# Input projection of a hybrid decoder layer: the left 240 token columns of each slot in two matmuls per K tile instead of three, with a VectorE add

## The chip, the cores and the metric

The kernel runs on one core of one Trainium2 chip, as one launch. The metric is the device time of a launch in microseconds (us). Before the change, three runs took 860.97, 862.88 and 862.4 us, a median of 862.4 us.

## The reference, cut to what matters

One decoder layer over 512 prompt tokens and 8 decode tokens, width 1024. The change touches only the first product, the input projection, whose columns feed an attention branch (q, k, v) and an RWKV branch:

```python
def token_mixer(x, x_prev_row, k_cache, v_cache, wkv0, w_in, ...):
    x_ext = jnp.concatenate([x_prev_row[:, None, :], x], axis=1)
    proj = x_ext @ w_in
    cur = proj[:, 1:]
    q = cur[..., :ATT_WIDTH]...; k = ...; v = ...
    rw_cur = cur[..., 3 * ATT_WIDTH:]
    rw_prev = proj[:, :-1, 3 * ATT_WIDTH:]
    rw = rw_cur + (rw_prev - rw_cur) * mu_shift
```

All tensors are fp32. Everything behind it (attention, the RWKV scan, output projection, layer norms, the convolutional FFN) is left alone.

## The kernel before

Activations lie channel-major: 128 channels on the partitions, tokens along the free dimension. The input projection works on `XC` = 528 token columns (512 prompt, 8 decode and their 8 previous rows) and `KT` = 8 K tiles. It goes through `N_IN` = 27 **slots**; a slot is one tile of 128 output channels. `SLOTS` sets the order: "a" slots give an attention tile, written to `att`; "r" slots give an RWKV tile, written to `pre` and then mixed with its neighbour column by `shift` into `rw`.

fp32 accuracy is had from the fast type fp32r by splitting both operands: `w_hi` is the weight rounded to fp32r by ScalarE, `w_lo` the rest, made by VectorE (`w_low`); `x_hi` and `x_lo` are the same for the activations. Each product is the sum of three: w_hi x_hi + w_hi x_lo + w_lo x_hi. A slot's 528 columns are two halves of 264; a half takes 8 K tiles of 3 matmuls of 264 columns, all accumulated in one PSUM bank (`banks[:, g % 3]`, g = 2 * slot + half). So the projection is 27 x 2 x 8 x 3 = 1296 matmuls.

What sets the order: every engine runs its own list, written by hand as loops over the slot number s, and the lists meet at semaphores.

- TensorE: `in_product(s)` runs the left half, then the right half. Between K tiles, `beside(half, i)` slips in small work of other stages: `scores`, `probs_t`, `values` (attention), `v_tokens` (slots 10, 12, 16, 20: transposes of the v tile), `low_rank`, `key_sums`, `key_spread`. A half waits until the bank that it takes over has been copied out (`in_copied`), and a slot for `w_lo` (`w_lo_ready`).
- ScalarE: in iteration s it copies out the right half of slot s-1 (`evac(s - 1, 1)`), makes `w_hi` of slot s+1, does the attention's copies, copies out the left half of slot s (`evac(s, 0)`), and then the exponentials (`att_exp`).
- VectorE: in iteration s it runs `shift(s - 1)` if that slot is an "r" slot, `w_low(s + 1)`, `mix_lo` every fourth slot, and then what belongs to the slot: `decay_sums`, `key_norm`, and from slot 10 on `soft` (score scaling and maxima) and `scale` (softmax division), with `transform` in slots 10, 14, 18 and 22. An iteration starts when the one before has ended: the engine is in order.

The SyncE list streams weights; it is not near the limit here. The small matmuls in `beside` use plain fp32; only the split products use fp32r.

Of the kernel before, what the change touches and what calls it, by code (L numbers as in the profile page):

```python
# [27 lines left out]
CC = AW // P  # L28
XC = T + 2 * B
XH = XC // 2  # L30
TC = T + B
TH = TC // 2
ALPHA = 2.0 ** 0.25
# [122 lines left out]
def layer(nc, a):  # L156
# [59 lines left out]
    onemka = sb(mixer, "onemka", [P, CC])  # L216

    pa = ExitStack()
    x_hi = sb(pa, "x_hi", [P, KT, XC], F32R)
    x_lo = sb(pa, "x_lo", [P, KT, XC], F32R)  # L220
    ksq = sb(pa, "ksq", [P, 2, XC])
    edec = ksq[:, :, 0:NCH * (CH + 1)].rearrange("p i (n t) -> p i n t", n=NCH)
    kbig = sb(pa, "kbig", [P, XC])
# [103 lines left out]
    w_hi_ready = sem("w_hi_ready")  # L327
    w_lo_ready = sem("w_lo_ready")
    w_late_ready = sem("w_late_ready")
    slot_used = sem("slot_used")  # L330
    sel_landed = sem("sel_landed")
    half_used = sem("half_used")
    const_landed = sem("const_landed")
# [3 lines left out]
    x_hi_ready = sem("x_hi_ready")  # L337
    x_lo_ready = sem("x_lo_ready")
    in_copied = sem("in_copied")
    rw_ready = sem("rw_ready")  # L340
    pre_zero = sem("pre_zero")
    v_tok_ps = sem("v_tok_ps")
# [181 lines left out]
    def _(sp):  # L524
# [72 lines left out]
        for s in range(2, N_IN):  # L597
            if s in (16, 20, 24):
                bias(s // 2 - 6)
                bias(s // 2 - 5)  # L600
            weights(s)
            if s == 6:
                sp.wait_ge(lora_ps, CC)
                sp.dma_start(low_up[:], a["bsel"]).then_inc(bsel_landed, 16)
            if s == 25:
                sp.wait_ge(in_copied, 2 * v_slots[-1] + 2)
                sp.dma_start(a["att_out"], att[:, CC:3 * CC, :]).then_inc(att_left, 16)

        sp.wait_ge(n_spread, CC)
# [2 lines left out]
        sp.wait_ge(w_lo_ready, N_IN)  # L612
        for v in range(2):
            sp.dma_start(swk[64 * v:64 * v + 64], a["swkv"][:, 32 * v:32 * v + 32, :]).then_inc(wkv_landed, 16)
        sp.wait_ge(slot_used, N_IN)
        sp.wait_ge(rw_ready, N_RW)
        sp.wait_ge(qb_done, 4 * CC)
        sp.wait_ge(a_mix_hi, CC)
# [72 lines left out]
    @block.gpsimd  # L691
    def _(pool):
        own = settled(pool)
        def w_low(l):
            n, s = k_tiles(l), N_IN + l
            hi, lo = w_at(l)
            pool.wait_ge(w_hi_ready, s + 1)
            pool.tensor_tensor(lo[:, 0:n * P], w_raw[:, s % 2, 0:n * P], hi[:, 0:n * P].bitcast(F32), ALU.subtract)\  # L698
                .then_inc(w_late_ready, 1)
            own(w_late_ready)  # L700

        pool.memset(pre[:, :, 0:1], 0.0).then_inc(pre_zero, 1)
        own(pre_zero)

        pool.wait_ge(slot_used, N_IN)
        for r in range(NKV):
            pool.memset(kv[96:P, r * NSB * AW:(r + 1) * NSB * AW], 0.0).then_inc(kv_zero, 1)  # L707
            own(kv_zero)

        def products(b):  # L710

            r = b % NKV
            pool.wait_ge(kv_landed[r], 64 * (b // NKV + 1))
            pool.wait_ge(q_landed[b % 2], 16 * (b // 2 + 1))
            rows = kv[:, r * NSB * AW:(r + 1) * NSB * AW].rearrange("p (t n) -> p t n", t=NSB)
            pool.tensor_tensor(rows, rows, qs[:, b % 2, :].unsqueeze(1).broadcast_to([P, NSB, AW]), ALU.mult)\
                .then_inc(q_used, 1)
            own(q_used)
            x = kv[:, r * NSB * AW:(r + 1) * NSB * AW].rearrange("p (g d) -> p g d", d=HD)
            pool.tensor_tensor(x[:, :, 0:HD // 2], x[:, :, 0:HD // 2], x[:, :, HD // 2:HD], ALU.add).then_inc(s_prod, 1)  # L720
            own(s_prod)

        def keys(q):
            return svec[:, q, :].unsqueeze(1).broadcast_to([P, 32, HD])

        def vals(x):
            return x.unsqueeze(2).broadcast_to([P, 32, HD])

        def step(out, a0, a1, op):
            pool.tensor_tensor(out, a0, a1, op).then_inc(sw_a, 1)  # L730
            own(sw_a)

        for b in range(NKV):
            products(b)
        pool.wait_ge(wkv_landed, 32)
        pool.wait_ge(sv_landed, 12 * 16)
        step(swt[:, :, :], swk, keys(4), ALU.mult)
        step(swk, swk, keys(1), ALU.mult)
        for b in range(NKV, B):
            products(b)  # L740
        pool.wait_ge(sw_sa, 1)
        step(swt[:, :, :], vals(ssa[:, 0, :]), keys(5), ALU.mult)
        step(swk, swk, swt[:, :, :], ALU.subtract)
        step(swt[:, :, :], vals(sval[:, :]), keys(2), ALU.mult)
        step(swk, swk, swt[:, :, :], ALU.add)
        step(swt[:, :, :], swk, keys(0), ALU.mult)

        def gate_parts(u):

            pool.wait_ge(gn_gs, u + 1)  # L750
            if u >= 2:
                pool.wait_ge(gn_o, u - 1)
            if u == 1:
                pool.wait_ge(s_sum, 1)
            w = P if u < TB else B
            pool.tensor_tensor(unit(gw_gate[:, u % 2, 0, :], u), unit(gsb, u),
                               par[:, C_GW:C_GW + CC].unsqueeze(2).broadcast_to([P, CC, w]), ALU.mult).then_inc(gn_g, 1)
            own(gn_g)
            pool.tensor_tensor(unit(gw_gate[:, u % 2, 1, :], u), unit(gsb, u), unit_of(rw[:, J_V:J_V + CC, :], u), ALU.mult)\
                .then_inc(gn_g, 1)  # L760
            own(gn_g)

        def odd_low(half, i):

            pool.wait_ge(ln_hi, KT * half + 2 * i + 2)
            pool.wait_ge(ln_zv, 2 * half + i // 2 + 1)
            x = slice(2 * i, 2 * i + 2)
            pool.tensor_tensor(x1_lo[:, x, span(half)], z[:, x, span(half)], x1_hi[:, x, span(half)].bitcast(F32),
                               ALU.subtract).then_inc(ln_lo_odd, 1)
            own(ln_lo_odd)  # L770

        pool.wait_ge(y_landed, 32)
        w_low(0)
        w_low(1)
        pool.wait_ge(vb_done, CC)
        gate_parts(0)
        gate_parts(1)
        w_low(2)
        gate_parts(2)
        w_low(3)  # L780
        w_low(4)
        gate_parts(3)
        w_low(5)
        w_low(6)
        gate_parts(4)
        for l in range(7, L_FF + 2):
            w_low(l)
        odd_low(0, 1)
        odd_low(0, 3)
        w_low(10)  # L790
        w_low(11)
        odd_low(1, 1)
        odd_low(1, 3)
        for l in range(L_FF + RING, N_LATE):
            w_low(l)
# [3 lines left out]
    def _(ac):  # L799
        own = settled(ac)  # L800
        def w_high(s):
            ac.wait_ge(w_landed[s % 2], 16 * (s // 2 + 1))
            if s >= 2:
                ac.wait_ge(slot_used, s - 1)
            ac.activation(w_hi[:, s % 2, :], w_raw[:, s % 2, :], ACT.Copy).then_inc(w_hi_ready, 1)
            own(w_hi_ready)

# [32 lines left out]

        def evac(s, half):
            kind, i = SLOTS[s]
            if half == 0:
                ac.wait_ge(half_used, s + 1)
            else:
                ac.wait_ge(slot_used, s + 1)
            lo = half * XH
            if kind == "a":
                if half == 0:
                    ac.wait_ge(x_lo_ready, KT)  # L850
                out = att[:, i, lo:lo + XH]
            else:
                r = RW_SEQ.index(i)
                if r >= 2:
                    ac.wait_ge(rw_ready, r - 1)
                if r == 0:
                    ac.wait_ge(pre_zero, 1)
                out = pre[:, r % 2, 1 + lo:1 + lo + XH]
            ac.activation(out, banks[:, (2 * s + half) % 3, 0:XH], ACT.Copy).then_inc(in_copied, 1)
            own(in_copied)  # L860

        def v_tok_copy(c):
# [143 lines left out]
        ac.wait_ge(ends_in, 2 * CC)  # L1006
        ac.activation(dec[:, :, :], dec[:, :, :], ACT.Exp, scale=DEC).then_inc(ends_done, 1)
        own(ends_done)
        ac.wait_ge(slot_used, N_IN)
        ac.wait_ge(a_mix_lo, CC)  # L1010
        rows_copy(0)
        x0_copy(0, 0)
# [222 lines left out]
    def _(ve):  # L1235
# [28 lines left out]
        link(ve.memset(kbig[:, 0:NCH * (CH + 1):CH + 1], 0.0))  # L1264
        link(ve.memset(cum[:, :, :, 0:1], 0.0))

        def shift(s):

            j = SLOTS[s][1]
# [73 lines left out]
        for s in range(N_IN + 1):  # L1343
            if s == 1:
                ve.wait_ge(const_landed, 16 * N_CONST)
                link(ve.tensor_scalar(onemka[:, :], par[:, C_KA:C_KA + CC], -1.0, 1.0, ALU.mult, ALU.add))
            if 1 <= s < N_IN and SLOTS[s - 1][0] == "r":
                shift(s - 1)
            if s + 1 < N_IN:
# [160 lines left out]
            ve.tensor_reduce(ssa[:, i, :], swt[:, :, :], AX, ALU.add).then_inc(sw_y if i else sw_sa, 1)  # L1510
            own(sw_y if i else sw_sa)

        ve.wait_ge(slot_used, N_IN)
        mix_lo(CC - 1)
        ve.wait_ge(ends_done, 1)
        inverse_start(0, 0)
# [362 lines left out]
    def _(pe):  # L1879
# [3 lines left out]
        def in_product(s, beside):  # L1883

            pe.wait_ge(w_lo_ready, s + 1)
            for half in range(2):
                g = 2 * s + half
                if g >= 3:
                    pe.wait_ge(in_copied, g - 2)
                out, cols = banks[:, g % 3, 0:XH], slice(half * XH, (half + 1) * XH)  # L1890
                for i in range(KT):
                    wh, wl = (w[:, s % 2, i * P:(i + 1) * P] for w in (w_hi, w_lo))
                    if g < 2 and i % 2 == 0:
                        pe.wait_ge(x_lo_ready, 4 * g + i // 2 + 1)
                    mm(out, wh, x_hi[:, i, cols], i == 0, False)
                    mm(out, wh, x_lo[:, i, cols], False, False)
                    ins = mm(out, wl, x_hi[:, i, cols], False, i == KT - 1)
                    if i < KT - 1:
                        beside(half, i)
                ins.then_inc(slot_used if half else half_used, 1)  # L1900

        def v_tokens(c):

            pe.wait_ge(in_copied, 2 * v_slots[c] + 2)
            if c == 0:
                pe.wait_ge(kk_ap, CC)
            else:
# [377 lines left out]
            ins.then_inc(bt_ps, 1)  # L2285

        pe.wait_ge(in_copied, 2 * N_IN)
        pe.wait_ge(a_biased, UNITS)
        pe.wait_ge(a_pt, UNITS)
        pe.wait_ge(a_mix_hi, CC)  # L2290
# [529 lines left out]
```

## Time and profile before

| | us |
|---|---|
| three runs, median | 862.4 |
| lowest and highest | 860.97, 862.88 |
| span of the profiled execution, first to last instruction | 860.4 |
| TensorE busy in the span | 807.1 (94%) |
| VectorE busy | 503.3 (58%) |
| ScalarE busy | 327.3 (38%) |
| input projection: its first and last matmul | 7.7 to 220.2 |
| TensorE busy from 8 to 222 | 211.7 of 214 |
| VectorE busy from 8 to 222 | 149.7 of 214 |
| TensorE busy, chunked recurrence, 222 to 380 | 131.1 of 158 |
| TensorE busy, output projection and FFN, 380 to 840 | 455.7 of 460 |

The times of the profile come from one execution, whose span is 2.0 us below the median of the runs. A matmul's recorded duration holds its way through the array and overlaps its neighbours', so the cost of a matmul in a row of equal ones is the distance between starts, not the duration. Plain fp32 matmuls leave two records each (8 calls of `key_spread`'s shape leave 16), fp32r matmuls one (1296 records for 1296 calls).

### The profile page before, as it was taken

What the parts mean: (1) busy time and instruction counts of PE and PEld (TensorE: products, weight loads), DVE (VectorE), ACT (ScalarE), POOL (GpSimd) and SP (SyncE); (2) the same over time, 40 slices, a digit from 0 to 9 for tenths busy, and PEclk for the clock granted to TensorE, in tenths of its full rate; (3) what the DMA queues carried; (4) which work ended last, traced back from release to release, by engine and by line L of the source; (5) the groups of instructions that cost most, each with busy time, mean ns of one, the idle gap of its engine ahead of it and who ended that gap; (6) DMA issues with size and microseconds to landing.
All of it is one profiled execution on the core that took longest, in us unless ns stands there. A gap on an engine that the chain in (4) does not pass through costs nothing.

```text
span 860.4 us, 23033 instructions
## 1 busy us (share of the span) xinstructions
PE 807.1 (94%) x9952; PEld 753.9 (88%) x9952; DVE 503.3 (58%) x779; ACT 327.3 (38%) x562; POOL 274.5 (32%) x121
## 2 busy tenths in 40 slices
PE   6999999999897777899999999999999999999994
PEld 6899898888776666689888999999999999999993
DVE  5588766687467667256466777776667661000046
ACT  5644465554312321534244434433333331111134
POOL 0000000000199490317143444444344434344410
PEclk9999999999999999999999999999999999999997
DMA  7222132143153323813111332322322322332202
GB/s 272 83 99 72 52 99 83 66 176 86 54 129 112 118 83 114 263 43 106 59 50 50 105 115 101 97 78 97 99 92 81 98 90 89 93 90 90 86 3 99
DMA packets 32469, 83.25 MB, mean 97 GB/s; under 512 B 5144, under 2 KB 10584, under 8 KB 31728
## 3 DMA queue, kind: packets, MB, share of 16 engines
q1 hardware_dynamic: 32368, 81.79, 30.5%
q8 instruction: 78, 1.28, 0.6%
q14 instruction: 23, 0.19, 0.1%
HBM read 75.67 MB, written 5.91 MB: 95 GB/s over the span
## 4 chain that ended last, share of the span: by engine, by line
PE 88%; DVE 7%; ACT 3%; issue 2%; DMA 0%; POOL 0%; DVEq 0%; ACTq 0%; POOLq 0%
PE banks L1881 85%; PE banks L1935 1%; ACT z L1218 1%; DVE xx L1246 1%; DVE ms L1246 1%; PE banks L2284 1%; DVE rw L1246 1%; DVE z L1246 1%; DVE ssa L1510 1%; DVE lower L1246 0%; DMA w_raw<-in_w 0%; ACT x_hi L1151 0%; DVE sscore L1479 0%; PE banks L1910 0%; DVE w_lo L1246 0%
## 5 line engine op out<-in xcount | busy, mean ns | idle before, releaser
L1881 PE MATMUL banks<-x_hi,w_hi 128*128 128x264 f32 (+1 forms) x784 | 206.3, 296 | 9.7 <-DVE x_lo L1246 7.7
L1881 PE MATMUL banks<-x_hi,w_lo 128*128 128x264 f32 (+1 forms) x784 | 197.3, 285 | 0.0
L1881 PE MATMUL banks<-x_lo,w_hi 128*128 128x264 f32 (+1 forms) x784 | 197.1, 285 | 0.0
L1881 PEld LDWEIGHTS banks<-x_hi,w_hi 128*128 128x128 f32 x784 | 137.8, 190 | 22.4 <-issue 11.3
L698 POOL TENSOR_TENSOR w_lo<-w_raw,w_hi 128x1024 fp32r<-128x1024 f32 (+1 forms) x38 | 90.8, 2390 | 150.6 <-ACT w_hi L827 150.3
L1881 PEld LDWEIGHTS banks<-x_lo,w_hi 128*128 128x128 f32 x784 | 137.9, 190 | 0.2
L1881 PEld LDWEIGHTS banks<-x_hi,w_lo 128*128 128x128 f32 x784 | 137.8, 190 | 0.0
L698 POOL TENSOR_TENSOR wx_lo<-w_raw,wx_hi 128x1024 fp32r<-128x1024 f32 (+1 forms) x34 | 81.4, 2395 | 99.8 <-ACT wx_hi L827 99.4
L1249 DVE SCALAR_TENSOR_TENSOR z<-z,banks 128x260 f32<-128x260 f32 (+1 forms) x24 | 12.4, 516 | 121.6 <-PE banks L1881 121.2
L707 POOL MEMSET kv<- 32x1536 f32 x3 | 4.1, 1373 | 219.8 <-PE banks L1881 219.7
L1881 PE MATMUL banks<-x_hi,wx_hi 128*128 128x260 f32 x352 | 73.6, 283 | 0.0
L1881 PE MATMUL banks<-x_hi,wx_lo 128*128 128x260 f32 x352 | 73.5, 283 | 0.0
L1881 PE MATMUL banks<-x_lo,wx_hi 128*128 128x260 f32 x352 | 73.4, 283 | 0.0
L1881 PE MATMUL banks<-xx,lower 64*64 64x64 f32 x1280 | 52.7, 226 | 17.2 <-DVE xx L1246 13.2
L1881 PEld LDWEIGHTS banks<-xx,lower 64*64 64x64 f32 x1280 | 45.8, 138 | 25.0 <-issue 12.3
L1249 DVE SCALAR_TENSOR_TENSOR cv<-gp,par,cv 128x544 f32<-128x544 f32 x44 | 66.0, 1500 | 1.6
L1246 DVE TENSOR_TENSOR h_lo<-hh,h_hi 128x520 fp32r<-128x520 f32 x22 | 51.5, 2339 | 23.5 <-ACT h_hi L1192 23.5
L827 ACT ACTIVATE w_hi<-w_raw 128x1024 fp32r<-128x1024 f32 (+1 forms) x38 | 39.5, 1039 | 45.4 <-PE banks L1881 44.6
L1881 PEld LDWEIGHTS banks<-x_hi,wx_hi 128*128 128x128 f32 x352 | 55.4, 188 | 0.0
L1881 PEld LDWEIGHTS banks<-x_hi,wx_lo 128*128 128x128 f32 x352 | 55.4, 188 | 0.0
L1881 PEld LDWEIGHTS banks<-x_lo,wx_hi 128*128 128x128 f32 x352 | 55.2, 188 | 0.0
L827 ACT ACTIVATE wx_hi<-w_raw 128x1024 fp32r<-128x1024 f32 (+1 forms) x34 | 35.2, 1037 | 45.8 <-PE banks L1881 45.0
(256 smaller groups left out, 1710.1 us busy)
## 6 DMA issues: line engine op xcount, KB each, us to landing
w_raw<-in_w SPq DMA_DIRECT2D x87, 512.0 KB, 3.6
w_raw<-in_w SPq DMA_DIRECT2D x16, 448.0 KB, 3.3
kv<-in_ck SPq DMA_DIRECT2D x16, 192.0 KB, 3.9
kv<-in_cv SPq DMA_DIRECT2D x16, 192.0 KB, 5.2
att<-in_x SPq DMA_DIRECT2D x8, 264.0 KB, 5.5
att_out<-att SPq DMA_DIRECT2D x1, 2112.0 KB, 9.0
z<-in_xc SPq DMA_DIRECT2D x2, 1040.0 KB, 7.9
y_out<-z SPq DMA_DIRECT2D x8, 260.0 KB, 2.2
```

Source lines behind the costliest of these rows:

```text
L698: pool.tensor_tensor(lo[:, 0:n * P], w_raw[:, s % 2, 0:n * P], hi[:, 0:n * P].bitcast(F32), ALU.subtract)\
L707: pool.memset(kv[96:P, r * NSB * AW:(r + 1) * NSB * AW], 0.0).then_inc(kv_zero, 1)
L827: ac.activation(w_at(l)[0][:, 0:n * P], w_raw[:, s % 2, 0:n * P], ACT.Copy).then_inc(w_hi_ready, 1)
L1218: ac.activation(z[:, c, span(half)], z[:, c, span(half)], ACT.Identity, bias=col(C_L2B + c)).then_inc(ln_z, 1)
L1246: return ve.tensor_tensor(out, a0, a1, op)
L1249: return ve.scalar_tensor_tensor(out, a0, s, a1, op0, op1)
L1510: ve.tensor_reduce(ssa[:, i, :], swt[:, :, :], AX, ALU.add).then_inc(sw_y if i else sw_sa, 1)
L1881: return pe.matmul(out, l, r, start=start, stop=stop)
L1935: ins = pe.transpose(banks[:, 4 - p, j * P:(j + 1) * P], sw[:, u % 4, j * P:(j + 1) * P], ident[:, :])
L2284: ins = pe.transpose(banks[:, 6, c * P:(c + 1) * P], x[:, c, n * P:n * P + P], ident[:, :])
```

## The change

The left part of a slot becomes `XL` = 240 columns, the right part `XR` = 288. `x_lo` and `x_hi` become two planes of one tile `x2`. In the left part, w_hi x_lo and w_hi x_hi are one matmul of 480 columns whose moving operand is the two pieces of 240; its two results lie side by side in the bank. w_lo x_hi is a matmul of 240 columns onto the second of them. The right part is as before with 288 columns. A left K tile has 2 matmuls, a right one 3: 27 x 8 x 5 = 1080 matmuls, 216 fewer, with the same 1584 moving columns per slot and K tile.

ScalarE copies the second result out (240 columns), and VectorE then adds the first from PSUM (`add_small`, a new step at the head of its iteration s, for slot s-1), counted by a new semaphore `in_summed`. TensorE waits for it before it takes a bank again, before each `v_tokens`, and at the end of the projection. `half_used` now counts both halves and stands for `slot_used` too.

```diff
+XL = 240
+XR = XC - XL
...
-    x_hi = sb(pa, "x_hi", [P, KT, XC], F32R)
-    x_lo = sb(pa, "x_lo", [P, KT, XC], F32R)
+    x2 = sb(pa, "x2", [P, 2, KT, XC], F32R)
+    x_lo, x_hi = x2[:, 0], x2[:, 1]
...
+            cols = (slice(0, XL), slice(XL, XC))[half]
...
+            o = (slice(XL, 2 * XL), slice(0, XR))[half]
+            ac.activation(out, banks[:, (2 * s + half) % 3, o], ACT.Copy).then_inc(in_copied, 1)
...
+        def add_small(s):
+
+            kind, i = SLOTS[s]
+            ve.wait_ge(in_copied, 2 * s + 1)
+            x = att[:, i, 0:XL] if kind == "a" else pre[:, RW_SEQ.index(i) % 2, 1:1 + XL]
+            tt(x, x, banks[:, 2 * s % 3, 0:XL], ALU.add).then_inc(in_summed, 1)
+            own(in_summed)
...
+            if s >= 1:
+                add_small(s - 1)
             if 1 <= s < N_IN and SLOTS[s - 1][0] == "r":
                 shift(s - 1)
...
                 if g >= 3:
                     pe.wait_ge(in_copied, g - 2)
-                out, cols = banks[:, g % 3, 0:XH], slice(half * XH, (half + 1) * XH)
+                    pe.wait_ge(in_summed, (g - 3) // 2 + 1)
+                b = g % 3
...
-                    mm(out, wh, x_hi[:, i, cols], i == 0, False)
-                    mm(out, wh, x_lo[:, i, cols], False, False)
-                    ins = mm(out, wl, x_hi[:, i, cols], False, i == KT - 1)
+                    if half == 0:
+                        mm(banks[:, b, 0:2 * XL].rearrange("p (a t) -> p a t", a=2), wh, x2[:, :, i, 0:XL], begin, False)
+                        ins = mm(banks[:, b, XL:2 * XL], wl, x_hi[:, i, 0:XL], False, end)
+                    else:
+                        mm(banks[:, b, 0:XR], wh, x_hi[:, i, XL:XC], begin, False)
+                        mm(banks[:, b, 0:XR], wh, x_lo[:, i, XL:XC], False, False)
+                        ins = mm(banks[:, b, 0:XR], wl, x_hi[:, i, XL:XC], False, end)
...
             pe.wait_ge(in_copied, 2 * v_slots[c] + 2)
+            pe.wait_ge(in_summed, v_slots[c] + 1)
```

TensorE's list at the end of the left half of slot 11 and the start of its right half, before:

```order
L1935 MATMUL banks<-ident,sw 128x128 [waits a_norm]
L1881 MATMUL banks<-x_hi,w_hi 128x264
L1881 MATMUL banks<-x_lo,w_hi 128x264
L1881 MATMUL banks<-x_hi,w_lo 128x264
L1881 MATMUL banks<-x_hi,w_hi 128x264 [waits in_copied]
```

The same place in the changed kernel (`x` is the tile `x2`):

```order
L1953 MATMUL banks<-ident,sw 128x128 [waits a_norm]
L1892 MATMUL banks<-x,w_hi 128x480
L1892 MATMUL banks<-x,w_lo 128x240
L1892 MATMUL banks<-x,w_hi 128x288 [waits in_summed,in_copied]
```

The last K tile of the left half has two matmuls in place of three, and the first matmul of the right half also waits for the add of slot 10.

VectorE's list from `transform` in iteration 10 to the weights' low part in iteration 12, before:

```order
L1246 TENSOR_TENSOR rw<-rw,ksq 128x512 [waits qb_done]
L1246 TENSOR_TENSOR w_lo<-w_raw,w_hi 128x1024 [waits w_hi_ready,qb_done]
L1249 SCALAR_TENSOR_TENSOR sw<-banks,abias 128x256 [waits a_scores,b_landed0,w_lo_ready]
...
L1295 TENSOR_SCALAR sw<-sw,rinv 128x256 [waits dve_chain]
L1246 TENSOR_TENSOR w_lo<-w_raw,w_hi 128x1024 [waits w_hi_ready,a_norm]
```

The same stretch in the changed kernel:

```order
L1247 TENSOR_TENSOR rw<-rw,ksq 128x512 [waits qb_done]
L1247 TENSOR_TENSOR att<-att,banks 128x240 [waits in_copied,qb_done]
L1247 TENSOR_TENSOR w_lo<-w_raw,w_hi 128x1024 [waits w_hi_ready,in_summed]
...
L1304 TENSOR_SCALAR sw<-sw,rinv 128x256 [waits dve_chain]
L1247 TENSOR_TENSOR att<-att,banks 128x240 [waits in_copied,a_norm]
```

An add stands at the head of each iteration, behind all that the iteration before had to do; nothing else has changed places.

## Rows read from the trace of the kernel before

**Rows 1.** The page: busy time, and the chain that ended last, by engine.

```profile
PE 807.1 (94%) x9952; PEld 753.9 (88%) x9952; DVE 503.3 (58%) x779; ACT 327.3 (38%) x562; POOL 274.5 (32%) x121
PE 88%; DVE 7%; ACT 3%; issue 2%; DMA 0%; POOL 0%; DVEq 0%; ACTq 0%; POOLq 0%
```

**Rows 2.** Timeline, TensorE, slot 2 (start, duration): first and last of 23 matmuls.

```profile
25.87 0.28 PE L1881 MATMUL banks<-x_lo,w_hi 128*128 128x264 f32 x1
...
28.55 0.28 PE L1881 MATMUL banks<-x_hi,w_lo 128*128 128x264 f32 x1
```

**Rows 3.** Windows, FFN: length, busy and count of PE, PEld, DVE, ACT, POOL.

```profile
480.00:700.00 220.00, 220.00 (x1834) 220.00 (x1833) 156.18 (x161) 82.61 (x118) 98.63 (x40) 1.00 0.31 96
```

**Rows 4.** Timeline, TensorE, slot 0: first and last of 22 matmuls.

```profile
8.06 0.42 PE L1881 MATMUL banks<-x_lo,w_hi 128*128 128x264 f32 x1
...
12.68 0.42 PE L1881 MATMUL banks<-x_lo,w_hi 128*128 128x264 f32 x1
```

**Rows 5.** Timeline, TensorE: plain fp32, 264, then 8 moving columns, merged.

```profile
66.73 1.05 PE L1881 MATMUL banks<-kbig,low_up 128*128 128x264 f32 x4
...
404.68 1.85 PE L1881 MATMUL banks<-rw,gate_up 128*128 128x8 f32 x16
```

**Rows 6.** One record's duration of these two (least, median, most ns).

```profile
L1881 PE MATMUL banks<-kbig,low_up x16: 383/386/386, 66.7 to 75.6; 128*128 128x264 f32 x16
...
L1881 PE MATMUL banks<-rw,gate_up x80: 175/275/377, 358.6 to 406.3; 128*128 128x128 f32 x64, 128*128 128x8 f32 x16
```

**Rows 7.** Timeline, VectorE: products of a PSUM and an SBUF operand.

```profile
221.69 0.69 DVE L1246 TENSOR_TENSOR mixa_lo<-banks,mixa_hi 128x512 fp32r<-128x512 f32 x1 [7.09 <-ACT mixa_hi L887]
...
231.09 0.42 DVE L1246 TENSOR_TENSOR lower<-banks,level 128x256 f32<-128x256 f32 x1 [0.39 <-DVE lower L1246]
```

**Rows 8.** Timeline, VectorE, end of iteration 5.

```profile
54.08 0.15 DVE L1318 TENSOR_SCALAR dec<-carry 128x1 f32<-128x1 f32 x1
```

**Rows 9.** Timeline, TensorE: first matmul of the right half of slot 6.

```profile
55.39 0.28 PE L1881 MATMUL banks<-x_hi,w_hi 128*128 128x264 f32 x1
```

**Rows 10.** Timeline, VectorE, slots 8 to 12.

```profile
67.89 0.71 DVE L1246 TENSOR_TENSOR rw<-rw,banks 128x528 f32<-128x528 f32 x1 [0.64 <-PE banks L1881]
...
85.49 0.16 DVE L1294 RECIPROCAL rinv<-rsum 128x1 f32<-128x1 f32 x1 [1.01 <-ACT sw L873]
...
89.52 0.69 DVE L1246 TENSOR_TENSOR rw<-rw,ksq 128x512 f32<-128x512 f32 x1
90.25 1.22 DVE L1246 TENSOR_TENSOR w_lo<-w_raw,w_hi 128x1024 fp32r<-128x1024 f32 x1
...
94.30 0.35 DVE L1295 TENSOR_SCALAR sw<-sw,rinv 128x256 f32<-128x256 f32 x1
```

**Rows 11.** Timeline, TensorE: right half of slot 11 starts; transposes of slots 12, 16.

```profile
90.51 0.28 PE L1881 MATMUL banks<-x_hi,w_hi 128*128 128x264 f32 x1
...
94.71 0.66 PE L1910 MATMUL banks<-ident,att 128*128 128x128 f32 x4 [0.18 <-ACT att L859]
...
128.43 0.66 PE L1910 MATMUL banks<-ident,att 128*128 128x128 f32 x4 [0.18 <-ACT att L859]
```

**Rows 12.** Timeline, VectorE, end of iteration 15.

```profile
127.20 0.35 DVE L1295 TENSOR_SCALAR sw<-sw,rinv 128x256 f32<-128x256 f32 x1
```

**Rows 13.** The chain that ended last, in order of time, slots 22 and 23.

```profile
189.86 0.72 DVE rw L1246
190.60 0.78 DVE rw L1249
191.41 1.24 DVE w_lo L1246
192.67 0.70 DVE mixa_lo L1246
193.50 5.34 PE banks L1881 x38
```

More of the change, by code:

```diff
@@ L329, in layer @@
     w_late_ready = sem("w_late_ready")
-    slot_used = sem("slot_used")
     sel_landed = sem("sel_landed")
@@ L339, in layer @@
     in_copied = sem("in_copied")
+    in_summed = sem("in_summed")
     rw_ready = sem("rw_ready")
@@ L606, in _ @@
                 sp.wait_ge(in_copied, 2 * v_slots[-1] + 2)
+                sp.wait_ge(in_summed, v_slots[-1] + 1)
                 sp.dma_start(a["att_out"], att[:, CC:3 * CC, :]).then_inc(att_left, 16)
@@ L614, in _ @@
             sp.dma_start(swk[64 * v:64 * v + 64], a["swkv"][:, 32 * v:32 * v + 32, :]).then_inc(wkv_landed, 16)
-        sp.wait_ge(slot_used, N_IN)
+        sp.wait_ge(half_used, 2 * N_IN)
         sp.wait_ge(rw_ready, N_RW)
@@ L703, in _ @@
         own(pre_zero)
-        pool.wait_ge(slot_used, N_IN)
+        pool.wait_ge(half_used, 2 * N_IN)
         for r in range(NKV):
@@ L803, in w_high @@
             if s >= 2:
-                ac.wait_ge(slot_used, s - 1)
+                ac.wait_ge(half_used, 2 * s - 2)
             ac.activation(w_hi[:, s % 2, :], w_raw[:, s % 2, :], ACT.Copy).then_inc(w_hi_ready, 1)
@@ L842, in evac @@
             kind, i = SLOTS[s]
[L843 to L847, printed above, removed]
+            ac.wait_ge(half_used, 2 * s + half + 1)
+            cols = (slice(0, XL), slice(XL, XC))[half]
             if kind == "a":
@@ L850, in evac @@
                     ac.wait_ge(x_lo_ready, KT)
-                out = att[:, i, lo:lo + XH]
+                out = att[:, i, cols]
             else:
@@ L857, in evac @@
                     ac.wait_ge(pre_zero, 1)
-                out = pre[:, r % 2, 1 + lo:1 + lo + XH]
-            ac.activation(out, banks[:, (2 * s + half) % 3, 0:XH], ACT.Copy).then_inc(in_copied, 1)
+                out = pre[:, r % 2, 1:1 + XC][:, cols]
+            o = (slice(XL, 2 * XL), slice(0, XR))[half]
+            ac.activation(out, banks[:, (2 * s + half) % 3, o], ACT.Copy).then_inc(in_copied, 1)
             own(in_copied)
@@ L1008, in _ @@
         own(ends_done)
-        ac.wait_ge(slot_used, N_IN)
+        ac.wait_ge(half_used, 2 * N_IN)
         ac.wait_ge(a_mix_lo, CC)
@@ L1511, in state_sum @@
             own(sw_y if i else sw_sa)
-        ve.wait_ge(slot_used, N_IN)
+        ve.wait_ge(half_used, 2 * N_IN)
         mix_lo(CC - 1)
@@ L1894, in in_product @@
                         pe.wait_ge(x_lo_ready, 4 * g + i // 2 + 1)
-                    mm(out, wh, x_hi[:, i, cols], i == 0, False)
-                    mm(out, wh, x_lo[:, i, cols], False, False)
-                    ins = mm(out, wl, x_hi[:, i, cols], False, i == KT - 1)
+                    begin, end = i == 0, i == KT - 1
+                    if half == 0:
[5 more added lines that the diff above has]
+                        ins = mm(banks[:, b, 0:XR], wl, x_hi[:, i, XL:XC], False, end)
                     if i < KT - 1:
                         beside(half, i)
-                ins.then_inc(slot_used if half else half_used, 1)
+                ins.then_inc(half_used, 1)
         def v_tokens(c):
             pe.wait_ge(in_copied, 2 * v_slots[c] + 2)
+            pe.wait_ge(in_summed, v_slots[c] + 1)
             if c == 0:
@@ L2287, in _ @@
         pe.wait_ge(in_copied, 2 * N_IN)
+        pe.wait_ge(in_summed, N_IN)
         pe.wait_ge(a_biased, UNITS)
```

## The prediction

> **What bounds the kernel now.** I read the page's busy shares and its chain first: TensorE is busy 94% of the span and makes up 88% of the chain that ended last [rows 1], so the time is TensorE's and what it waits for. Then the timeline of the projection. A matmul costs the distance between starts: 23 matmuls of 264 columns from 25.87 to 28.55 are 22 steps of 121.8 ns [rows 2]. In the FFN some 1831 matmuls of 260 columns fill 220 us (1834 records touch the window, three of them at its edges): 120.1 ns each [rows 3]. The 1.7 ns between the two are four columns at 2.4 GHz (0.417 ns each). So a warm fp32r matmul is N/2.4 plus 11.8 ns, at both lengths: 110.0 + 11.8 and 108.3 + 11.8. The projection is 1296 such steps, and around them sit the small matmuls, which the change leaves alone.
>
> **What TensorE saves.** A K tile of a slot now costs 6 x 121.8 = 730.8 ns. After the change it has one matmul of 480, one of 240 and three of 288 columns, together the same 1584 columns. With 11.8 ns on each: 211.8 + 111.8 + 3 x 131.8 = 719.0 ns. That is 11.8 ns less, times 216 K tiles: **-2.5 us**. No row shows fp32r at 480, 240 or 288 columns, so each has bounds.
>
> - 480: the nearest row in moving time is a plain fp32 record of 264 columns, which takes 220 ns, as much as 528 columns at full clock. Four records in 1.05 us with 386 ns for the last [rows 5, 6] are 221.3 ns apart, 1.3 ns over the columns. So 201.3 to 211.8 ns. In slot 0, at the lower clock level of 1.2 GHz, fp32r steps of 264 columns are (12.68 - 8.06)/21 = 220.0 ns [rows 4], with nothing on top. Both say that what is added may vanish when the columns take 200 ns. Against it stands that it didn't shrink between 260 and 264. I take 211.8, the value at full clock in this type.
> - 240: with only 8 moving columns and a full 128 x 128 weight load per record, 16 records take 1.85 us, (1.85 - 0.175)/15 = 111.7 ns apart [rows 5, 6]. That is the pace of the loads, a lower bound for any full matmul. Upwards nothing in fp32r lies below 260 columns; the plain fp32 matmul, 2 x 221.3 = 442.6 ns at 264, gives 2 x 201.3 = 402.6 at 240. I take 111.8, since 260 columns are the nearest row.
> - 288: 121.3 to 131.8; I take 131.8.
>
> So a left half of 8 K tiles gets 24 x 121.8 - 8 x 323.6 = 334 ns shorter, a right half 8 x 395.4 - 24 x 121.8 = 240 ns longer, a slot 94 ns shorter. The first K tiles, in the lower clock, go by the same columns and are no exception worth a term. The moving operand of 480 columns comes in two pieces of 240; no row has such a split in fp32r, and I put nothing on it.
>
> **What the adds cost VectorE.** An add of 240 columns with one operand in PSUM: 0.42 us at 256 columns and 0.69 at 512 [rows 7], so 0.41, with some 0.04 to the next instruction 0.45 us. 27 of them are 12 us of VectorE, which has 64 us free from 8 to 222. ScalarE's copies change from 264 + 264 to 240 + 288 columns: nothing. SyncE and GpSimd are past no new work; the wait before the v output DMA and the one at the projection's end are met long before, since VectorE idles 7.09 us ahead of its last step there [rows 7].
>
> What matters is where an add comes late. It stands behind all of iteration s-1, and TensorE wants it at the right half of slot s (now 0.33 us earlier than before) and at `v_tokens`. Most iterations end 3 to 5 us ahead. The tight places:
>
> - Slot 6. Iteration 5 ended at 54.23 [rows 8], the right half started at 55.39 [rows 9]. Two adds in this unbroken stretch (0.90) and 0.33 for the shorter left half use up the 1.16, and TensorE's own gains until then do the rest: a stall of 0.15 to 0.3.
> - Slots 8 to 12. From 67.89 VectorE has no gap of note but 1.01 at 85.49 [rows 10]. The adds of slots 8 and 9 fall ahead of that gap and mostly fill it. Iteration 10 ended at 90.21 and TensorE started the right half of slot 11 at 90.51 [rows 11], a slack of 0.30; 0.45 and 0.33 exceed it. Then iteration 11 ended at 94.65, and the transposes of slot 12, at 94.71 before, now wait for the adds of slots 10 and 11: the base is 94.65, plus 0.90 for the two, less the some 0.4 by which this chain starts earlier (it hangs on TensorE's `key_spread` in slot 8), so 95.2 against 94.71. TensorE would have been there about 1.1 us earlier than before: 11.5 slots x 0.094. **Stalls of 1.6 us** in slots 10 to 12, with the wait at 94.71 of 0.18 in them.
> - Slots 16 and 20: iteration 15 ended at 127.55 [rows 12], the transposes came at 128.43 [rows 11] because of ScalarE's copy. Two adds make it 128.45, and TensorE is 0.15 earlier within these slots. 0.2 each, **0.4**.
> - Slot 23: here VectorE is in the chain already: shift, w_lo, mixa_lo, then TensorE at 193.50 [rows 13]. The add of slot 22 goes ahead of the shift, so it is on the path in full: **0.45**.
>
> Sum: -2.5 + 0.2 + 1.6 + 0.4 + 0.45 = about **+0.1 us**, on a span of 860.4; carried to the median of the runs, 2.0 us above that span, 862.5 us. If the cover of the other adds were gone, all 27 would be 12.2 us, so the change would cost 9.6.
>
> **Rivals.** (B) What is added per matmul fades for longer columns. For it: rows 4 and 5. Against: rows 2 and 3. In full, a K tile is 201.3 + 112 + 3 x 121.3 = 677.2 ns, 53.6 less, 11.6 us in all; if only the 480 gains, 708.5 ns, 22.3 less, 4.8 us. VectorE's tight places take back more, since it doesn't get faster with TensorE: 4 to 6 us in place of 2.6 in the full case, so 862.4 - 11.6 + (4 to 6), 855 to 857; in the partial one 862.4 - 4.8 + 3, 860.6. I take 856 as its time. The Trainium skill (TensorE: Matmul & The Clock Gate, Back-to-back issue gap) gives a sustained spacing of some 81 ns at 128 columns and 131 at 512, by which long matmuls are far cheaper per column. By an estimate on the line between these, a K tile would fall from 592 to 528 ns and the change would gain 13.9 us before stalls. The trace speaks against it: 260 columns take 120.1 ns here, where that line has 98.
>
> (C) The waits for VectorE cost more than I count. The place is slots 8 to 12 and 23, the price 0.45 per add, and it decides when the exponentials or the weights' low part become late as well, so that three to six more adds land on the path: +1.4 to +2.7, and if the 288-column halves then meet `mix_lo` late in slots 15 and 19 too, +3.6. 865.
>
> (D) The 240-column matmul leaves the fast rate and runs as plain fp32 does. For it: nothing in the trace, but also no fp32r matmul under 260 columns to exclude it, and the type is known here only at 260 and 264. Against: 240 is near. It is decided by that one shape; the price is 402.6 - 111.8 = 290.8 ns x 216 = +62.8 us. The stalls go (VectorE then has time), so 862.4 - 2.5 + 62.8 = 923.
>
> **How the numbers follow.** Forecast 0.46 (862.5, by itself 860.5 to 864.5), B 0.22, C 0.15, D 0.17. The measurement can tell about 0.2%, 1.7 us, from no change. Faster: B but for its partial end, and the forecast's lower edge, 0.27. Slower: C, D and the upper edge, 0.34. Same: 0.39. The range leaves out D and the far end of B: 855 to 867.
>
> **What would show it.** In the profile after: steps of 212, 112 and 132 ns for the three shapes (B: 201 and 121; D: about 400 for the 240). A left half without other work of 2.59 us, a right one of 3.16. VectorE adds of 0.41 us, TensorE waits on them only at slots 6, 11, 12, 16, 20, and mixa_lo in slot 23 later by 0.45 relative to TensorE. The stage from 222 on is unchanged in length. The prediction is wrong if any of the three shapes has another step, since 1 ns on a K tile is 0.2 us, or if waits for VectorE sum to more than 4 us.

## The result and the profile after

The changed kernel took **870.09 us** (median of 6 runs, 867.08 to 876.39), the kernel before on the same chip 863.31 (6 runs, 860.97 to 864.45): a ratio of 1.0085, 95% interval [1.0057, 1.0112]. It is **slower**, by 0.85% as that ratio has it and by 6.8 us (0.79%) as the medians do. The forecast was 862.5 in a range of 855 to 867, and its weightiest case was "no change", so the forecast was wrong and the range too.

The page of the changed kernel, in the order of the pages above: busy time and instructions of each engine, the transfers that bring in the instructions, and the chain that ended last, by engine.

```profile
PE 811.6 (93%) x9736; PEld 748.1 (86%) x9736; DVE 514.3 (59%) x806; ACT 327.0 (38%) x562; POOL 274.7 (32%) x121
q8 instruction: 77, 1.26, 0.6%
PE 86%; DVE 7%; ACT 5%; issue 2%; DMA 0%; POOL 0%; DVEq 0%; ACTq 0%; POOLq 0%
```

TensorE has 216 matmuls and 216 weight loads less than in [rows 1] and is busy 4.5 us longer. VectorE has 27 instructions and 11.0 us more, as intended. These averages don't say where 7.8 us of span (868.2 against 860.4) were lost. Windows of three stretches do: projection, recurrence (the stage from 223 us on), the rest. The columns are length, busy time and count of TensorE, its weight loads, VectorE, ScalarE and GpSimd, then TensorE's granted clock (1.00 is 2.4 GHz), DMA share and GB/s. The kernel before:

```profile
7.00:222.00 215.00, 211.95 (x1696) 192.72 (x1696) 150.65 (x266) 111.05 (x217) 1.37 (x1) 1.00 0.32 102
223.00:375.00 152.00, 125.70 (x3941) 106.53 (x3933) 94.74 (x178) 45.88 (x96) 81.00 (x29) 0.99 0.43 129
```

The changed kernel:

```profile
7.00:222.00 215.00, 211.51 (x1480) 183.23 (x1480) 161.20 (x292) 110.29 (x215) 0.75 (x1) 1.00 0.32 101
223.00:375.00 152.00, 123.10 (x3772) 103.91 (x3776) 88.98 (x169) 41.51 (x83) 81.60 (x29) 0.96 0.43 128
```

In the first stretch the changed kernel has done its 216 matmuls fewer, and all else of TensorE's work alike. In the second, in the same 152 us, it gets 169 matmuls less far, at a lower granted clock. That stretch of the program is the same in both kernels. Its first matmul and the first `gsq,hsel` matmul, near its end, in the kernel before:

```profile
222.63 1.16 PE L1881 MATMUL banks<-rw,aa 64*64 64x64 f32 x64 [2.18 <-DVE mixa_lo L1246]
366.98 0.42 PE L1881 MATMUL banks<-gsq,hsel 128*32 128x128 f32 x8
```

and in the changed one:

```profile
223.32 1.99 PE L1892 MATMUL banks<-rw,aa 64*64 64x64 f32 x64 [2.20 <-DVE mixa_lo L1247]
374.91 0.43 PE L1892 MATMUL banks<-gsq,hsel 128*32 128x128 f32 x8
```

The recurrence begins 0.7 us later and then takes 151.6 us where it took 144.35: **7.2 us of the 7.8 are lost in a stage that the change doesn't touch.** After it the two run 7.9 us apart and stay so.

**The projection itself.** TensorE's timeline in slot 2, seven left K tiles without other work and, further on, five right ones:

```profile
29.69 0.38 PE L1892 MATMUL banks<-x,w_hi 128*128 128x480 f32 x1
29.91 0.27 PE L1892 MATMUL banks<-x,w_lo 128*128 128x240 f32 x1
...
31.67 0.38 PE L1892 MATMUL banks<-x,w_hi 128*128 128x480 f32 x1
...
33.98 0.43 PE L1892 MATMUL banks<-x,w_hi 128*128 128x288 f32 x2
...
35.58 0.30 PE L1892 MATMUL banks<-x,w_hi 128*128 128x288 f32 x1
```

A left K tile is (31.67 - 29.69)/6 = 330 ns, of which the 480 columns have 220 and the 240 columns 110. A right one is (35.58 - 33.98)/4 = 400 ns, 133 for each 288. Together 730 ns where 6 x 121.8 [rows 2] made 730.8: **the merge saves next to nothing**.

The stalls for the adds stand where the prediction put them, at the transposes of slot 12 and in slot 23:

```profile
94.63 0.40 DVE L1247 TENSOR_TENSOR att<-att,banks 128x240 f32<-128x240 f32 x1
95.14 0.63 PE L1928 MATMUL banks<-ident,att 128*128 128x128 f32 x4 [0.52 <-ACT att L860]
...
190.04 0.42 DVE pre L1247
190.48 0.72 DVE rw L1247
...
193.29 0.70 DVE mixa_lo L1247
```

The transposes come at 95.14 after 94.71 with a wait of 0.18 [rows 11]. The profile puts the wait down to ScalarE's copy, but that ended at 94.80 and the add of slot 11, the row above, at 95.03: TensorE waited for the add. The lower three rows are the chain: the add of slot 22 (0.42 us) now stands in it ahead of the shift, and `mixa_lo` starts at 193.29 after 192.67 [rows 13].

**Waits with nothing behind them.** The waits of TensorE in the recurrence, by what ended them (us in total, times, longest), before:

```profile
PE banks L1881 <- DVE xx L1246: 13.2, 11, 2.7
PE banks L1881 <- issue: 6.7, 7, 2.1
```

and after:

```profile
PE banks L1892 <- DVE xx L1247: 11.0, 10, 2.7
PE banks L1892 <- issue: 8.3, 9, 2.1
```

"issue" is time in which no semaphore holds TensorE. Such a wait looks like this in the timeline of the changed kernel, in a run of small matmuls that need nothing new:

```profile
298.00 0.28 PE L1892 MATMUL banks<-xx,lower 64*64 64x64 f32 x2
300.36 0.27 PE L1892 MATMUL banks<-xx,lower 64*64 64x64 f32 x1 [2.09 <-issue]
```

and what came after it, in a window from 302 to 305:

```profile
302.00:305.00 3.00, 3.00 (x94) 2.97 (x92) 1.07 (x3) 0.00 (x0) 2.94 (x1) 0.50 0.00 0
```

TensorE is busy all the time there, at 1.2 GHz. In the recurrence the stretches at 1.2 GHz sum to 3.4 us before and 13.6 us after.

### The profile page after: what moved, and what is told of

Its sections match the earlier page's. It is cut to its first block, busy times and chain, and to the rows that moved or that the text cites. A ratio compares the mean times of both kernels' runs of the same rounds, so it can differ in the third digit from the quotient of the medians.

```text
span 868.2 us, 22682 instructions
## 1 busy us (share of the span) xinstructions
PE 811.6 (93%) x9736; PEld 748.1 (86%) x9736; DVE 514.3 (59%) x806; ACT 327.0 (38%) x562; POOL 274.7 (32%) x121
## 4 chain that ended last, share of the span: by engine, by line
PE 86%; DVE 7%; ACT 5%; issue 2%; DMA 0%; POOL 0%; DVEq 0%; ACTq 0%; POOLq 0%
PE banks L1892 83%; DVE rw L1247 1%; ACT z L1219 1%; PE banks L1953 1%; DVE xx L1247 1%; PE banks L2302 1%; DVE ms L1247 1%; ACT nv L985 1%; DVE z L1247 1%; DVE ssa L1521 1%; DMA w_raw<-in_w 0%; ACT w_hi L830 0%; ACT x_hi L1152 0%; DVE lower L1247 0%; DVE w_lo L1247 0%
## 5 line engine op out<-in xcount | busy, mean ns | idle before, releaser
L1892 PE MATMUL banks<-x,w_hi 128*128 128x288 f32 (+1 forms) x648 | 171.1, 339 | 7.8 <-DVE x L1247 7.6
L1892 PEld LDWEIGHTS banks<-x,w_hi 128*128 128x128 f32 x648 | 110.3, 190 | 25.1 <-issue 11.9
L1892 PE MATMUL banks<-x,w_lo 128*128 128x240 f32 (+1 forms) x432 | 123.7, 286 | 0.0
L1892 PEld LDWEIGHTS banks<-x,w_lo 128*128 128x128 f32 x432 | 82.6, 191 | 0.1
L1892 PE MATMUL banks<-x_hi,w_hi 128*128 128x260 f32 x352 | 74.2, 285 | 1.9 <-POOL x_lo L771 1.9
L1892 PE MATMUL banks<-x_hi,w_lo 128*128 128x260 f32 x352 | 73.5, 283 | 0.0
L1892 PE MATMUL banks<-x_lo,w_hi 128*128 128x260 f32 x352 | 73.4, 283 | 0.0
L1892 PEld LDWEIGHTS banks<-x_hi,w_hi 128*128 128x128 f32 x352 | 55.3, 188 | 2.8 <-POOL x_lo L771 2.3
L1892 PEld LDWEIGHTS banks<-x_hi,w_lo 128*128 128x128 f32 x352 | 55.4, 188 | 0.0
```

The source lines that it names most:

```text
L1892: return pe.matmul(out, l, r, start=start, stop=stop)
```

## What was tried

Unless said otherwise each kernel was timed over 10 or 12 runs beside the kernel before on the same chip. "Theory T4" and the like are the names in the expectations.

**1. The merge alone, without the adds.** Relative to the changed kernel:

```diff
-            if s >= 1:
-                add_small(s - 1)
...
-                    pe.wait_ge(in_summed, (g - 3) // 2 + 1)
```

> The changed kernel without the VectorE adds and without every wait for them; the left 240 columns lack the w_hi x_lo part. From the two traces: the projection ended 0.7 us later than before and the rest of the 7.9 us of the span arose in the recurrence, where the profile of after has four periods at the 1.2 GHz level and that of before has one. Theory T1 (those periods come and go with the moment at which the recurrence's gaps fall, the projection itself matters little): the projection ends some 0.4 us earlier than before (27 slots x 0.014), the time is anywhere from 862 to 872, and the mean clock tells which. Theory T2 (the adds, by delaying TensorE, are the cause): 862.5 to 863, clock as before. Theory T3 (the merged matmuls, with fewer weight loads, are the cause): 869 to 871.

867.67 us, ratio 1.003 [1.0011, 1.005]. The recurrence begins at 222.27, 0.4 us earlier than before, and takes 153.0 us.

**2. The adds alone**, with three matmuls of 264 columns in each half as before:

```diff
+XL = 264
...
+            tt(x[:, 0:240], x[:, 0:240], banks[:, 2 * s % 3, 0:240], ALU.max).then_inc(in_summed, 1)
```

> The three matmuls of 264 columns per half as before, with VectorE's step over 240 columns (a maximum of the copied value and the bank, so that nothing is left out) and every wait for it. Predicted stalls: 0.2 at slot 6, 1.6 in slots 10 to 12, 0.4 at 16 and 20, 0.45 at 23, less 0.33 at each right half since the left half isn't shorter: about 1.7 us in the projection. T1: 1.7 us plus whatever the clock does, 864 to 872. T2: 870. T3: 865, clock as before.

865.78 us, ratio 1.0025 [1.0005, 1.0045]. The recurrence begins at 224.15, 1.5 us later than before, and takes 146.6 us.

**3. The split alone**, 240 and 288 columns, three matmuls each, no adds:

```diff
-                        mm(banks[:, b, 0:2 * XL].rearrange("p (a t) -> p a t", a=2), wh, x2[:, :, i, 0:XL], begin, False)
+                        mm(banks[:, b, XL:2 * XL], wh, x_hi[:, i, 0:XL], begin, False)
+                        mm(banks[:, b, XL:2 * XL], wh, x_lo[:, i, 0:XL], False, False)
```

> Three matmuls in both parts, but parts of 240 and 288 columns; no adds, nothing left out. It prices the split alone. With N/2.4 + 11.8: a slot is 24 x (111.8 + 131.8) = 5846 ns, the same as before, projection unchanged, 863. If 240 is at the pace of the loads (111.7) and 288 has 13 ns over its columns: +0.03 us a slot, +0.8 us. T1: within 862 to 872 by the clock; T2 and T3: 863 to 864.

865.34 us, ratio 1.0009 [0.9991, 1.0027]. Start 223.04, recurrence 148.6 us. Against the first kernel it has the matmul count of the kernel before, a projection 0.8 us longer, and yet it isn't slower. So the loss in the recurrence goes with the missing matmuls.

**4. The kernel before with the recurrence held back** by two VectorE copies:

```diff
+            if c == CC - 1:
+                link(ve.tensor_copy(tmp[:, :], kbig[:, :]))
+                link(ve.tensor_copy(tmp[:, :], kbig[:, :]))
```

> The kernel before with two VectorE copies of 528 columns (together about 1 us) ahead of mixa_lo at the end of the projection, so that TensorE starts the recurrence about 1 us later and nothing else changes. T1: more than the 1 us is lost in at least some runs, because the gap at the start of the recurrence gets longer and its place changes: 865 to 872, lower mean clock. T2 and T3: 864.3, clock as before.

867.13 us, ratio 1.0024 [1.0006, 1.0042]. It starts at 224.76, 2.1 us late, and the median is up by 2.6 us, or 2.1 by the ratio: the delay itself and nothing beyond it. That the moment of the start decides (T1) found no support, and T2 leaves out the first kernel, which has no adds. T3 (the merged matmuls) comes nearest, but put that kernel at 869 to 871, above its 867.67, and names no mechanism.

**A new theory.** The trace also records the transfers by which a core gets its instructions, 16384 bytes each. By their number they are TensorE's: the page counts 78 before and 77 after, and the trace has 20,137 instructions of TensorE before and 19,731 after (matmuls, loads, and 233 and 259 semaphore instructions), which are 78.7 and 77.1 blocks of 256. Set beside TensorE's large waits in the recurrence without a releaser, they read (worked out from the trace; us):

```
changed kernel                         kernel before
transfer          wait                 transfer          wait
242.29 to 243.42  243.52 to 244.96     278.27 to 279.63  280.20 to 281.23
271.47 to 272.56  272.58 to 273.87     284.39 to 285.32  285.69 to 286.73
298.11 to 299.07  298.27 to 300.36     309.51 to 310.49  310.68 to 311.94
329.79 to 330.72  331.62 to 332.14     323.35 to 324.28  324.78 to 325.57
348.58 to 349.56  348.96 to 350.92     346.33 to 347.25  346.82 to 348.94
```

Every wait ends 1.3 to 1.7 us after a transfer has landed. Over all 18 profiles of this study there are 127 such waits of 0.3 us or more, and every one ends 1.15 to 1.71 us after a landing (median 1.40), although the transfers are some 5 us apart in this stage: a moment picked at random would do so one time in nine. The last pair, as the profile has it: the transfer's row in a 0.1 us window from 348.5, then the matmul that it let go, both of the changed kernel:

```profile
q8 instruction: 1, 0.02, 61.6%
...
350.92 0.27 PE L1892 MATMUL banks<-ms,vt 64*64 64x64 f32 x2 [1.96 <-issue]
```

Where these waits stand in TensorE's list decides it. With all its instructions in the trace numbered from 0, semaphore instructions included, the matmul behind each of the 127 waits has a number that is 193 or 194 modulo 256. So they all stand at the same place of a 256-instruction block, and there TensorE runs out of instructions until the next block is in. It doesn't do so at every block: the recurrence has some 30 of them and 5 to 10 such waits.

A projection with 216 matmuls and 216 loads less moves everything behind it against these blocks: 432 fewer is, modulo 256, the same shift as 80 more. That can be tested without touching the computation. One thing is missing in this count, and in the expectations below: the changed kernel has 26 semaphore instructions more ahead of the recurrence (100 against 74), so its shift is 106 and not 80. Run 1, which lacks them, is at 80.

**5 to 8. Padding.** One-column matmuls ahead of slot 0, where TensorE waits 7.7 us anyway, each with its load:

```diff
+        def padding(n):
+            pe.wait_ge(pre_zero, 1)
+            x = pre[:, 0, 0:1].bitcast(mybir.dt.bfloat16)[:, 0:1]
+            for _ in range(n):
+                mm(banks[0:1, 7, 0:1], x, x)
+
+        padding(40)
```

> The kernel before, with 40 one-column matmuls (and their 40 loads) ahead of slot 0, where TensorE waits 7.7 us for its first operands anyway. They only move every later TensorE instruction by 80 places in its program. The trace fetches TensorE's program in transfers of 16384 bytes, and the changed kernel's 432 fewer instructions are the same shift as 80 more, taken modulo 256 of 64 bytes each. Theory T4 (the merge costs time in the recurrence because TensorE's program is shifted against its fetches): the waits without a visible releaser move to where the changed kernel has them (21, 50, 77 and 128 us into the recurrence) and the time rises by 2 to 6 us, to 866 to 870, with the projection as before. Rival T5 (the merged matmul itself or its heavier VectorE does it, positions do not matter): same as before, 863 to 864.5.

867.75 us, ratio 1.0037 [1.0019, 1.0054]. Recurrence 152.9 us. The kernel before, with nothing changed but its position, has about half of the loss (0.37 of 0.85%). Four of its eight waits, which end at 242.7, 274.3, 300.6 and 351.2, are within 2.3 us of where the changed kernel has them:

```profile
300.56 0.27 PE L1881 MATMUL banks<-xx,lower 64*64 64x64 f32 x1 [2.26 <-issue]
351.19 0.28 PE L1881 MATMUL banks<-vt,ktok 64*64 64x64 f32 x3 [2.80 <-issue]
```

> Control for the padding: the kernel before with 128 one-column matmuls and their 128 loads ahead of slot 0, a shift by 256 places, which is none modulo 256. T4: waits of TensorE in the recurrence stay where the kernel before has them, time as before (within 1 us, less whatever an earlier rise of the clock in slot 0 gives). T5: the same. If this one is slower by 2 us or more, padding costs something of its own and the first run says nothing.

864.3 us, ratio 0.9997 [0.9977, 1.0017]: the padding itself costs nothing. In its profile the recurrence takes 149.5 us, which is 5 more than in the one of the kernel before, so a single profile of this stage scatters by that much.

> The changed kernel with 88 one-column matmuls and their loads ahead of slot 0: 176 places, which with the 432 that the merge takes away make a shift of none modulo 256. T4: the waits return to the places of the kernel before (about 64, 89, 103 and 126 us into the recurrence), gsq,hsel comes 144 to 147 us after the recurrence begins instead of 151.6, and the time is 863 to 866. T5: as the changed kernel, 868 to 871.

865.93 us, ratio 1.0018 [1.0001, 1.0034]. Recurrence 147.0 us; four of its eight waits are back near those of the kernel before, at 282.7, 313.3, 327.1 and 351.8. The changed kernel, shifted back (to 26, not quite to 0), loses 2.0 us instead of 6.8.

> Control: the changed kernel with 128 one-column matmuls and their loads ahead of slot 0, no shift modulo 256. T4 and T5: both 868 to 871, as the changed kernel, the waits in the recurrence 21, 50, 77 and 128 us into it; so T4 wants this one 3 us or more above the 88-pair one on the same chip.

871.64 us (6 runs), ratio 1.0082 [1.0061, 1.0104], as the changed kernel has it: shifting by a whole block changes nothing, shifting by 80 less than that gains 5.7 us. It also has the longest of these waits:

```profile
358.01 0.37 PE L1892 MATMUL banks<-ms,vt 64*64 64x64 f32 x2 [4.95 <-issue]
```

**9. The 2.2 us ahead of the recurrence filled** with eight matmuls of 512 columns (120 one-column matmuls keep the position):

```diff
+        for _ in range(8):
+            mm(banks[:, 6, 0:512], mixa_hi[:, 0, 0:P], mixa_hi[:, 0, 0:512])
```

> The kernel before with eight 512-column fp32r matmuls on data already there, into a free bank, in the 2.2 us that TensorE waits between the projection and the recurrence (1.9 us by 0.22 us each), and 120 one-column matmuls ahead of slot 0, so that everything from the recurrence on stands 256 places later, which is no shift against the fetches. Theory T6 (TensorE's low clock costs time of its own where TensorE sets the pace: the wait is followed by 3.4 us at half clock in most profiles, at 223 us): with the wait filled the half clock at 223 is gone and the time is 1 to 1.7 us less than with the 128 one-column matmuls alone (864.3), 862.6 to 863.3. Rival (that stretch of the recurrence is paced by the other engines, or the half clock merely comes later): 864 to 865.

865.93 us, ratio 1.0016 [0.9995, 1.0037]. TensorE's idle time fell from 2.18 to 0.34 us, and the clock stayed at 2.4 GHz until 274 us, but it then ran at 1.2 GHz for 6.8 us on end; in all 13.6 us of the recurrence. What the filling did to the clock this single profile can't show: the kernel before, without it, kept 2.4 GHz until 272.6 us, and three of the padded ones below likewise until 272.6 to 273.8. Nothing gained: the rival expectation, or somewhat worse.

```profile
222.31 1.16 PE L1881 MATMUL banks<-rw,aa 64*64 64x64 f32 x64 [0.34 <-DVE mixa_lo L1246]
```

**10. 480 columns from one run of addresses:**

```diff
+                            mm(banks[:, b, 0:2 * XL], wh, x2[:, 0, i, 0:2 * XL], begin, False)
```

> The changed kernel with the 480 moving columns of slots 1 to 26 taken from one run of addresses (x_lo's own 480 columns) instead of two pieces of 240; what they multiply is not the reference's. A left K tile took 330 ns for 480 + 240 columns, the merged step some 220 ns. If the second piece is what puts the step 8 ns over N/2.4 + 11.8 ns, the K tile comes to 322 ns here and the left half to 2.58 us; if it is the size, 330 ns and 2.64 us remain. The time otherwise as the changed kernel, 867 to 871.

871.05 us (3 runs), ratio 1.0081 [1.0053, 1.0109]. From the sixth left K tile of slot 2 to the next:

```profile
30.66 0.38 PE L1892 MATMUL banks<-x,w_hi 128*128 128x480 f32 x1
...
30.99 0.38 PE L1892 MATMUL banks<-x,w_hi 128*128 128x480 f32 x1
```

330 ns, and 328 on the mean of the half. The two pieces cost 2 ns at most; the extra 8 ns belong to the size.

**11 to 16. Other positions**, by the same padding:

> The kernel before with 64 one-column matmuls ahead of slot 0: everything stands 128 places later against the fetches, half a transfer. Theory T4 (positions set the waits of the recurrence): the waits without a releaser come at other places than in any kernel so far, and the time differs from that with 128 of them (864.3); by how much is not worked out, since no run shows this position: 861 to 871. If it is 864 to 865 with the waits where the kernel before has them, T4 falls.

> The same with 96 one-column matmuls: 192 places later. T4: again other places, 861 to 871. With this one there are four positions (0, 80, 128, 192) of one and the same kernel; T4 says that the spread between them is 3 us or more, and that one of them can be below the kernel before.

> The kernel before with 112 one-column matmuls ahead of slot 0: 224 places later. Positions measured so far: 0 and 256 at 863.6 to 864.3 us, 80 at 867.8, 128 at 866.7, 192 at 863.5. T4 (position sets the recurrence's waits): lies between its neighbours, 863 to 865.

> The same with 80: 160 places later, between the positions that gave 866.7 and 863.5. T4: 863.5 to 867. Below 862 it would be the fastest kernel so far.

> The same with 20: 40 places later, between the positions that gave 863.9 and 867.8. T4: 864 to 868.

> The changed kernel with 56 one-column matmuls ahead of slot 0: 112 places later, less the 432 that the merge takes away, which is the position of the kernel before with 96 of them (192 places, 863.5 us). If position and the change's own cost add, it takes 2.0 us more than that one: 865.5 us, 864.3 to 867. If the changed kernel has a loss of its own in the recurrence that the 88-pair version hid by luck, 868 to 871.

Positions are counted in instructions of TensorE ahead of the recurrence, semaphore instructions included, against the kernel before, modulo 256:

| position | kernel before: us, ratio | changed kernel: us, ratio |
|---|---|---|
| 0 | 863.3 to 864.5 (unpadded), 1; 864.3, 0.9997 | |
| 26 | | 865.93, 1.0018 |
| 40 | 864.71, 1.0013 [0.9996, 1.0031] | |
| 80 | 867.75, 1.0037 [1.0019, 1.0054] | |
| 106 | | 870.09, 1.0085 (unpadded); 871.64, 1.0082 |
| 128 | 866.69, 1.0033 [1.0014, 1.0051] | |
| 160 | 863.62, 0.9988 [0.9970, 1.0006] | |
| 192 | 863.52, 0.9993 [0.9978, 1.0008] | |
| 218 | | 867.40, 1.0039 [1.0021, 1.0058] |
| 224 | 865.67, 1.0014 [0.9995, 1.0032] | |

The same computation spreads over some 4 us by its position alone. The five profiles at positions 80 and 106 (runs 1 and 5; the changed kernel and runs 8 and 10) have recurrences of 151.6 to 157.1 us, the thirteen at others 144.4 to 150.4: the two groups don't overlap. Position 224 came out at 865.67, above the 863 to 865 expected of it. No position of either kernel is measurably faster than the kernel before.

## Why the prediction was wrong, step by step

**The step that failed** is one sentence: "The stage from 222 on is unchanged in length." It took 7.2 us more in the profile. The prediction treated removing 216 matmuls as removing their time only. Removing them also moves the 7,900 TensorE instructions of the recurrence against the blocks in which instructions arrive. In the kernel before alone a shift of 80 costs 0.37% or **3.2 us** (1.6 to 4.7 by the interval) and one of 128 costs 2.9; the changed kernel's own, 106, lies between them. In the changed kernel the positions 106 and 26 are 5.5 us apart on one chip (1.0082 against 1.0018). No rival had it, though its material was in the trace of before: waits put down to "issue" in the recurrence, 6.7 us of them, with a transfer of instructions ahead of each.

How 7.2 us come about there is shown only in part. Some of it may be scatter between two single profiles: the profile of run 6 has 5 us more of recurrence than that of the kernel before, at the same position and with the same median time. The waits without a releaser sum to 7.3 us after and 6.2 before, so they alone give 1.1. The stretches at 1.2 GHz are 10.2 us longer; if TensorE sets the pace in them, half of that, 5.1 us, is lost (an estimate). That they follow such waits can be seen (300.36, then 302 to 305), but run 9 took one gap away and gained nothing. Over the 18 profiles the length of the recurrence goes with both, the sum of these waits (correlation 0.79) and the time at 1.2 GHz (0.83). So "waits at worse places, and a lower clock behind them" fits; what each is worth, and why one position is worse than another, stays open. So does what makes a transfer start when it does.

**The change's own price** was put at +0.1 us. No two runs of the two kernels stand at equal positions. By an estimate, on a straight line between the nearest two positions of the kernel before, the changed kernel is 0.9 us (position 26), 4.1 (106, padded) and 2.5 (218) above it, each uncertain by some 2 us. The last of the runs, expected at 864.3 to 867, gave 867.4; it was taken for position 192, but is at 218, near the slower 224. Whether position and own price simply add is not shown.

Of this price the projection accounts for 1.3 us. From the first matmul of slot 2 to that of slot 26, where the clock in slot 0 plays no part, all five profiles that have both merge and adds take 191.7 us, the kernel before 190.4, the merge alone 190.0 and the adds alone 191.9:

- **Saving: -2.5 us forecast, -0.2 (from 730 ns a K tile) to -0.4 (run 1) found.** The mis-sized term is the step of the merged matmul, 211.8 ns taken and 220 measured, outside the bounds of 201.3 to 211.8. What is added to N/2.4 is not 11.8 ns at the new lengths but 20 at 480 columns and 13 at 288. It grows, where rival B let it vanish. The 240 columns take 110 ns behind the 480, where 111.8 were forecast and 111.7 was called a lower bound. Per K tile 730 ns instead of 719. Run 1 shows it by itself: its projection ends 0.4 us earlier. Run 10 excludes the two pieces as the cause.
- **Stalls for the adds: +2.6 forecast, +1.7 found** (191.7 against the 190.0 of the merge alone). Run 2, where 1.7 were expected, has 1.5. An add takes 0.42 us as forecast, and the tight places were the right ones: slots 6, 10 to 12, and 23. In the changed kernel, from how starts shift against the kernel before, they cost about 0.2, 0.9 and 0.3 us; slots 16 and 20 cost nothing that can be seen.

-0.4 + 1.7 = +1.3 us, against +0.1. The recurrence of the changed kernel began only 0.7 us late, since slot 0 reached the full clock 1.4 us earlier in this profile (11.7 against 13.2 us), which is worth about half of that. What lies between this 1.3 and the estimates above, up to 3 us, may be scatter or positions that weren't measured; its place wasn't found.

**The rivals.** B (longer matmuls cheaper) is refuted by 220 ns for 480 columns. On this the Trainium skill (TensorE: Matmul & The Clock Gate, Back-to-back issue gap), with some 131 ns at 512 columns, doesn't fit the fp32r matmuls of this trace. D (240 columns at the plain fp32 rate) is refuted by 110 ns. C (more waits for VectorE) named a time near the result, 865, but not its cause: the stalls cost less than forecast, not more. The sum of projection terms was off by 1.2 us; the rest of the miss is the recurrence.

## What to carry to other kernels

A change in the number of instructions ahead of a stage of many small matmuls moves that stage against the blocks in which its instructions arrive; here that alone was worth up to 0.4%, as much as the change was meant to bring or more. Look in the trace of before for waits put down to "issue" beside instruction transfers, and if there are any, time both kernels at several positions (a few tiny matmuls where the engine waits anyway; semaphore instructions count too) before a gain or loss of under 1% is put down to the edit. And merging matmuls with the same columns in total only gains what is added per matmul, which has to be measured at the new size.

## What was unexpected of the hardware

- TensorE waits up to 4.95 us with no semaphore behind it while a 16384-byte block of instructions arrives. Each of 127 such waits ended 1.15 to 1.71 us after a block had landed, and all stand at the same place modulo 256 of its instruction list.
- The fp32r step over N/2.4 isn't constant: 10 ns at 240 columns (behind 480), 11.8 at 260 and 264, 13 at 288, 20 at 480, from one run of addresses too.
- Filling a gap of 2.2 us with dense matmuls gained no time (1.0016 [0.9995, 1.0037]); the clock fell to 1.2 GHz later in that stage, in all for 13.6 us.
